# Norm weights applied to rows, operands made in pieces, low-rank products two to a bank

## What is computed

```python
def rms_norm(x, g):
    y = xf * lax.rsqrt(jnp.mean(xf * xf, axis=-1, keepdims=True) + RMS_EPS)
    return (y * g).astype(x.dtype)

p = rms_norm(h, norm_mix_pre) @ w_in                  
r, k, v, wd, ad, gd = split(p_rw + (shift(p_rw) - p_rw) * mu)
w = -softplus(-(w0 + tanh(wd) @ w2)) - 0.5            # low-rank products
a = sigmoid(a0 + ad @ a2);  g = sigmoid(gd) @ g2
# 8 heads, state S[64 x 64]:  S = S*decay + sa (kk*a)^T + v k^T ;  y = S r
y = group_norm_heads(y) * lnx_w + lnx_b               # the recurrent rows
# retention: q, k rotated (rotary), 8 heads, two chunks of 128; group norm per head, silu gate
h = h + rms_norm(merged @ w_out, norm_mix_post)
h = h + rms_norm(conv_ffn(rms_norm(h, norm_ffn_pre)), norm_ffn_post)
# second block: mamba2 mixer, per-layer embedding, shared keys and values
# (kv_norm), window attention (attn_norm), per-layer embedding
```

## Time and profile before

| | |
|---|---|
| median of 3 runs | 992.21 us (991.54 to 994.03) |
| the profiled execution | 992.41 us, span 990.4 us |
| PE busy | 921.5 us (93%), mean granted clock 0.979 |
| DVE busy | 682.0 us (69%) |
| ACT busy | 518.2 us (52%) |
| POOL busy | 62.5 us (6%) |
| PE in the chain that ended last | 63% |
| bytes moved | 135.57 MB, 137 GB/s |

### The profile page before, as it was taken

One profiled execution on the slowest core, in us unless ns is written; L12 is line 12 of the kernel. 1 busy time (PEld: TensorE's weight loads), 2 busy tenths in 40 slices (PEclk: granted clock), 3 DMA queues, 4 the chain that ended last, 5 costly groups with the idle time before them and its releaser, 6 DMA issues.

```text
span 990.4 us, 14250 instructions
## 1 busy us (share of the span) xinstructions
PE 921.5 (93%) x5697; PEld 808.3 (82%) x5697; DVE 682.0 (69%) x936; ACT 518.2 (52%) x745; POOL 62.5 (6%) x65
## 2 busy tenths in 40 slices
PE   4989999999998997999999889989989998999988
PEld 3887898889886876999988689977878786778776
DVE  4569753793488668888873587877556776877654
ACT  4654331232454355666643465865556566467643
POOL 7000420440000000000000000000000000000000
PEclk9899999999999997999999979999999999999999
DMA  9432221222354443656555625543322444542231
GB/s 304 133 128 85 85 87 43 85 86 71 101 187 153 161 156 132 210 179 206 182 201 176 202 91 165 182 130 127 127 75 97 138 159 149 192 137 97 85 101 70
DMA packets 80530, 135.57 MB, mean 137 GB/s; under 512 B 3893, under 2 KB 46225, under 8 KB 80464
## 3 DMA queue, kind: packets, MB, share of 16 engines
q1 hardware_dynamic: 78640, 131.17, 40.2%
q0 software_dynamic: 1824, 3.48, 1.1%
HBM read 133.59 MB, written 1.05 MB: 136 GB/s over the span
## 4 chain that ended last, share of the span: by engine, by line
PE 63%; ACT 6%; DVE 5%; issue 3%; DMA 1%; ACTq 0%; DVEq 0%
PE bank L418 18%; PE bank L420 17%; PE bank L419 17%; PE bank L406 3%; ACT upper L1170 2%; DVE lower L1652 1%; PE bank L833 1%; PE bank L1027 1%; PE bank L842 1%; PE bank L1011 1%; ACT arena L1589 1%; ACT arena L1232 1%; PE bank L643 1%; DVE h L1711 1%; DMA loaded<-in_ffn_w_up 1%
## 5 line engine op out<-in xcount | busy, mean ns | idle before, releaser
L1652 DVE TENSOR_TENSOR lower<-loaded,upper 128x2048 fp32r<-128x2048 f32 (+1 forms) x123 | 279.3, 2276 | 131.5 <-ACT upper L1170 129.5
L1170 ACT ACTIVATE upper<-loaded 128x2048 fp32r<-128x2048 f32 (+1 forms) x123 | 233.7, 1901 | 113.5 <-PE bank L420 94.5
L418 PE MATMUL bank<-xT_upper,upper 128*128 128x256 f32 (+1 forms) x664 | 189.7, 286 | 9.0 <-DVE xT_lower L1693 9.0
L419 PE MATMUL bank<-xT_lower,upper 128*128 128x256 f32 (+1 forms) x664 | 188.1, 283 | 0.0
L420 PE MATMUL bank<-xT_upper,lower 128*128 128x256 f32 (+1 forms) x664 | 187.8, 283 | 0.0
L418 PE MATMUL bank<-upper,xT_upper 128*128 128x512 f32 x352 | 145.9, 414 | 6.2 <-DVE lower L1652 3.5
L420 PE MATMUL bank<-upper,xT_lower 128*128 128x512 f32 x352 | 138.9, 395 | 0.0
L419 PE MATMUL bank<-lower,xT_upper 128*128 128x512 f32 x352 | 138.2, 393 | 0.0
L418 PEld LDWEIGHTS bank<-xT_upper,upper 128*128 128x128 f32 (+1 forms) x664 | 128.7, 194 | 10.9 <-issue 10.8
L418 PE MATMUL bank<-upper,split_arena 128*128 128x512 f32 x296 | 121.2, 410 | 11.6 <-DVE arena L2193 4.7
L419 PEld LDWEIGHTS bank<-xT_lower,upper 128*128 128x128 f32 (+1 forms) x664 | 128.7, 194 | 0.1
(11 more groups left out here) (318 smaller groups left out, 1200.7 us busy)
## 6 DMA issues: line engine op xcount, KB each, us to landing
loaded<-in_w_in SPq DMA_DIRECT2D x27, 1024.0 KB, 5.1
loaded<-in_ffn_w_up SPq DMA_DIRECT2D x22, 1024.0 KB, 5.1
loaded<-in_ssm_in_w SPq DMA_DIRECT2D x20, 1024.0 KB, 5.3
loaded<-in_ffn_w_down SPq DMA_DIRECT2D x11, 1024.0 KB, 4.9
loaded<-in_ssm_out_w SPq DMA_DIRECT2D x8, 1024.0 KB, 4.9
loaded<-in_ple_gate_w SPq DMA_DIRECT2D x8, 1024.0 KB, 5.1
loaded<-in_attn_in_w SPq DMA_DIRECT2D x8, 1024.0 KB, 5.3
loaded<-in_w_branch_ret SPq DMA_DIRECT2D x4, 1024.0 KB, 5.0
```

The source lines that it names most:

```text
L418: mm(out, a[0], b[0], start=start, stop=False)
L419: mm(out, a[0], b[1], start=False, stop=False)
L1170: A(part(upper, PARTS, n), part(loaded, LOADS, n), ACT.Copy).then_inc(uppers, 1)
L1652: TT(part(lower, LOADS, n), part(loaded, LOADS, n), part(upper, PARTS, n).bitcast(F32), sub) \
```

## The change

1. Norms 1 and 2: the weight is broadcast over the partitions by two new transfers (`rowsw`), and applied to the rows, before the transpose (for the first tile by a product of `h` with it beside the sums, for the second within the scaling). `scale` goes; the halves are made straight from PSUM.
2. `pieces` names the banks and the blocks of 128 columns of each transposed tile; rows are scaled in halves, and PE waits for pieces of columns and not for halves of a tile.
3. Norm 0 and the key-value part of norm 4: ACT and DVE make the halves per block, straight from PSUM, with the weight as the column that scales it (`columns_upper`, `columns_lower`). The first unit is loaded and split in two halves, and the first product runs over both column groups half by half (`first_turned`). The square of norm 4 is taken in two halves.
4. The constant table is loaded after four units. The broadcasts of GpSimd's list stand behind its work on the first inverse.
5. Low-rank products of decay and rate: two to a bank, so four banks hold all eight; the gate's four go to four banks; ACT copies the gates before it widens `kroot`. `columns(4)` moves one unit earlier.
6. `L` products between the `m` products; angles in two calls; a rotation in two calls, its sum and weight behind the next level's adds; output copies of `dense` no longer three quarters behind at `L` and at the first scores.
7. The recurrent rows are centred tile by tile, between the right-hand sides and after the first scores; the first output tile's norm moves ahead of `dense("o")`.

The core of the diff:

```diff
+        def pieces(n, i):
+            if n in (3, 5):
+                banks = (2 * i, 2 * i + 1)
+            elif n == 4:
+                banks = (6, 7) if i else (4, 5, 0, 1)
+            elif n == 1:
+                banks = (2, 3, 6, 7) if i else (0, 1)
+            else:
+                banks = (6, 7, 2, 3) if i else (4, 5)
+            m = KT // len(banks)
+            return [(("nT", n, i, p), bank, m * p, m) for p, bank in enumerate(banks)]
...
 PE
+            def first_turned(name, keys):
+                for half in range(2):
+                    pe.wait_ge(lowers, half + 1)
+                    for c in range(2):
+                        for k in range(4 * half, 4 * half + 4):
+                            if c == 0:
+                                xT_ready(0, (5 if k < 4 else 9) + k)
+                            last = mm3(...)
...
+                    for q in range(2):
+                        for name, bank, r, x in (("w", 4, ...), ("a", 6, ...)):
+                            ps = take(pe, (name, q), bank + q)
+                            for e in range(2):
+                                last = mm(ps[:, T * e:T * e + T], ...)
...
-                        lora_product("g", p, 6 + p % 2, lora[:, 1, P * p:P * p + P], lor[:, 1, :])
+                        ps = take(pe, ("g", p), 4 + p)
...
+                    if hd in (3, 5):
+                        o = hd // 5          # the four products of ("L", n, o)
...
-                        if between and half and i == 0:
+                        if between and i and half == 0:
                             between()
...
 SP
-                if n == 2:
+                if n == LOADS:
                     sp.dma_start(consts[:, P:ncols], io["table"][:, P:ncols])
+                if n == 0:
+                    sp.dma_start(dst[:, 0:4, :], src[:, 0:4, :]).then_inc(sem("first_landed"), 16)
+                    sp.wait_ge(sem("x_landed0"), 16)
+                    sp.dma_start(dst[:, 4:8, :], src[:, 4:8, :]).then_inc(unit_landed[0], 16)
...
 GpSimd
             pool.dma_start(h[:, :, :], io["x"]...).then_inc(sem("x_again"), 16)
+            spread_row(rowsw[0], io["norm_ffn_pre"][0], "rowsw_landed0")
             pool.wait_ge(sem("h_ready"), 2)
             spread_row(postw[:, :], io["norm_ffn_post"][0], "postw_landed")
+            spread_row(rowsw[1], io["ssm_norm_w_2"][0], "rowsw_landed1")
...
 ACT
+            def columns_upper(n, x, w, i, first=0, last=4):
+                for key, _, k0, m in pieces(n, i)[first:last]:
+                    ps = full(act, key)
+                    for k in range(m):
+                        A(x[0][:, k0 + k, P * i:P * i + P], ps[:, P * k:P * k + P], ACT.Identity,
+                          scale=pc(w, k0 + k)).then_inc(sem("xT_upper_ready"), 1)
...
                 for i in range(2):
                     post_sums(key, m, i)
+                    if i:
+                        norm_upper(n, xT, (0,))
                     row_sums(n, i)
+                norm_upper(n, xT, (1,))
...
                         elif m == 0 and i == 0:
+                            first_sums(1)
                             root_table()
-                            row_sums(4, 0)
+                            other_sums(0)
+                            split_to("pg01.1", 1)
+                            columns_upper(4, xT2, "kv_norm_w_2", 0)
...
 DVE
             def post_norm(key, m, n, w):
                 post_rows(key, m, 0)
+                ve.wait_ge(sem(f"rowsw_landed{n - 1}"), 16)
+                ve.wait_ge(sem("h_ready"), 2 * n - 1)
+                link(TT(hs[:, 0, :], h[:, 0, :], w, mul))
                 row_scale(n, 0)
                 post_rows(key, m, 1)
-                scale(n, 0, xT, w)
-                row_scale(n, 1)
                 lower_rows(n, 0, xT)
-                scale(n, 1, xT, w)
+                ve.wait_ge(sem("h_ready"), 2 * n)
+                row_scale(n, 1, w)
                 lower_rows(n, 1, xT)
...
+                    if n and 1 < k < 6:
+                        rope_piece(k - 2, True)
                     dense(("t", n, k))
                     if n and k < 5:
-                        rope_piece(k - 1)
+                        rope_piece(k - 1, False)
                     dense(("x", n, k))
                     if n == 0 and k == 1:
                         angles()
+                    if n == 0 and k == 2:
+                        angles_left()
...
                 dense(("rhs", n))
+                if n:
+                    centre_recurrent(0)
...
                 dense(("scores", n))
+                if n == 0:
+                    centre_recurrent(1)
...
+            output_norm(0)
+            dense("o")
             for i in range(2):
                 ps = full(ve, ("yT", i))
```

More of the change, by code:

```diff
@@ L410, in norm_turns @@
                 for i in tiles:
-                    pe.wait_ge(sem("rows_scaled"), 2 * n + i + 1)
-                    for q in range(2):
-                        turns(("nT", n, i, q), (0 if n in (1, 3, 5) else 4) + 2 * i + q, [hs[:, i, P * (4 * q + j):P * (4 * q + j + 1)]
-                                                               for j in range(4)])
+                    for key, bank, k0, m in pieces(n, i):
+                        pe.wait_ge(sem("rows_scaled"), 2 * (2 * n + i) + (2 if k0 + m > 4 else 1))
+                        turns(key, bank, [hs[:, i, P * k:P * k + P] for k in range(k0, k0 + m)])
             def mm3(out, a, b, start, stop):
@@ L454, in turned @@
                     fill(last, keys[c])
+                used(name, key=keys[1])
+            def first_turned(name, keys):
+                ps = [take(pe, keys[c], c) for c in range(2)]
+                n = index[name]
+                w = tiles(part(upper, PARTS, n), n), tiles(part(lower, LOADS, n), n)
+                for half in range(2):
[4 more added lines that the diff above has]
+                                xT_ready(0, (5 if k < 4 else 9) + k)
+                            last = mm3(ps[c][:, 0:T], both(w, every, k, slice(c * P, c * P + P)), both(xT, every, k, every),
+                                       k == 0, k == KT - 1)
+                        if half:
+                            fill(last, keys[c])
                 used(name, key=keys[1])
@@ L1160, in _, with first_upper @@
             A = act.activation
-            split_at = [0]
+            split_at = [1]
+            def first_upper(half):
+                if half == 0:
+                    act.wait_ge(sem("first_landed"), 16)
+                else:
+                    act.wait_ge(unit_landed[0], 16)
+                c = slice(1024 * half, 1024 * half + 1024)
+                A(part(upper, PARTS, 0)[:, c], part(loaded, LOADS, 0)[:, c], ACT.Copy).then_inc(uppers, 1)
             def split_to(name, more=0):
@@ L1277, in _ @@
                 if m == 2:
+                    for q in range(2):
+                        for name, dst in (("w", ld), ("a", av)):
+                            ps = full(act, (name, q))
+                            for e in range(2):
+                                p = 2 * q + e
+                                ins = A(dst[:, p, :], ps[:, T * e:T * e + T], ACT.Sigmoid, bias=pc(f"rw_{name}0", p))
+                            empty(ins, (name, q))
                     for p in range(4):
@@ L1293, in _ @@
                 if m == 4:
+                    for p in range(4):
+                        copy(gT[:, p, :], ("g", p), T)
                     act.wait_ge(sem("knorm_ready"), 1)
@@ L1296, in _ @@
                         .then_inc(sem("knorm_wide"), 1)
-                    for p in range(4):
-                        copy(gT[:, p, :], ("g", p), T)
                 if m == 6:
@@ L1688, in lower_rows @@
+            def scale(n, i, x, w, r0=0):
+                for key, _, k0, m in pieces(n, i):
+                    ps = full(ve, key)
+                    g = cols[:, colat[(w, r0)] + k0:colat[(w, r0)] + k0 + m]
+                    TT(hs[:, i, P * k0:P * (k0 + m)].rearrange("p (a b) -> p a b", a=m),
+                       ps[:, 0:P * m].rearrange("p (a b) -> p a b", a=m), bc(g.unsqueeze(2), P, m, P), mul) \
+                        .then_inc(sem("xT_scaled"), 1)
             def lower_rows(n, i, x):
-                for q in range(2):
-                    xl[0] += 1
+                for key, _, k0, m in pieces(n, i):
+                    xl[0] += m
@@ new lines, in lower_rows, with columns_lower @@
+                    src = full(ve, key)[:, 0:P * m] if n in (1, 2) else hs[:, i, P * k0:P * (k0 + m)]
+                    TT(x[1][c], src.rearrange("p (a b) -> p a b", a=m), x[0][c].bitcast(F32), sub) \
+                        .then_inc(sem("xT_lower_ready"), m)
+                if n in (1, 2):
+                    ve.wait_ge(sem("xT_lower_ready"), 16 * n + 8 * i + 8)
+                for key, _, k0, m in pieces(n, i):
+                    empty(ve.nop(), key)
+            def columns_lower(n, x, w, i, first=0, last=4):
```

(9 more changed lines are left out.)

289 lines of the change are left out of this document (158 added, 131 removed).

## The result

The changed kernel took 965.25 us (median of 5 executions, 962.94 to 973.29), the kernel before 994.03 on the same chip (5, 991.54 to 995.33): a ratio of 0.972, with a 95% interval of 0.969 to 0.975. 960 with a range of 951 to 971 was forecast. The profiled execution is the slowest of the five, 973.29 with a span of 971.4; the others have spans of 961.2 to 963.8.

The account below looks back on a forecast made before the run. TensorE was taken to bound the kernel, busy 921.5 of 990.4 us, so edits pay only where it waits. Ten steps summed to 32.1 us saved from 992.4, giving 960.3 (960 from the median), range 951 to 971.

Parts of the forecast that it names:

- Start: Step 1: first product at 12.8 us instead of 18.76, by splitting half a unit and working in blocks; 6.3 us saved.
- Low-rank: Step 2: eight small products no longer wait for the column copy or for banks to be emptied; 6.0 us saved.
- Gates: Step 3: gate products on four banks instead of two, ending a 2.72 us wait; 3.7 us saved, bounds 1 and 4.
- Masks: Step 4: four-product groups put between the mask products remove waits of 1.00 and 1.38; 0.8 us saved.
- Inverse, scores, end of the recurrent part: Steps 5, 6, 7: waits removed at the inverse, score stage and late weight halves after the recurrent part; 4.0, 1.0, 5.0 us.
- The two norms: Step 8: norms after the feed-forward's input and output; 2.0 us saved twice between second h and first product, 4.0 together.
- Key-value norm: Step 9: blocks replace scaling, upper and lower at the key-value norm, its wait split in three; 1.0 us saved.
- The last: Step 10: row scaling in halves removes the last embedding's 0.36 us wait; 0.3 us saved.
- A: VectorE takes over, blocks and copies ending late in decay, mask and rotation stretches; 8.2 us less, 968; chance 0.20.
- B: TensorE's clock stays at 2.4 GHz at the two norms, where the forecast left it slow; 954 us; chance 0.12.
- C: TensorE's clock falls oftener as one long wait becomes several short ones; 997 us at mean 0.94; chance 0.02.
- D: The blocks do nothing, bank and semaphore order giving the same chains; only steps 2, 3, 8 work; 978 us; chance 0.05.

Follow-up runs that it names:

- after: The profiled execution of the unaltered changed kernel, the slowest of its five: 973.29 us, span 971.4.
- step 2 alone: Kernel before with only low-rank products two to a bank, sigmoids ahead of squares and the fourth column group one projection earlier: 987.88 us, ratio 0.997.
- the repeat: The changed kernel, unaltered, executed and profiled a second time: 963.29 us, ratio 0.972 to the kernel before; profiled span 958.8.
- the undone step: Changed kernel with the four gate products on two banks again: 967.73 us, ratio 0.974 to the kernel before.
- the later table: Changed kernel with the constant table issued after the fifth weight unit instead of after the fourth: 966.39 us, ratio 0.973 to the kernel before.
- the eleven fillers: Changed kernel with 11 identity products filling TensorE's wait at each of norms 1 and 2: 962.60 us, ratio 0.969 to the kernel before.
- the weights on columns: Changed kernel with the weights of norms 1 and 2 on the transposed columns again, in the new pieces: 970.57 us, ratio 0.976 to the kernel before.

## Why the prediction was right, step by step

Steps 1, 5, 6, 9 and 10 have no run of their own: the table places their gains, and their causes are read from the rows. The others were undone or made alone.

**Start (6.3).** Right in size: first product at 11.61 and, in eleven further traces of the changed start, at 11.5 to 13.3 (median of all 12.1), against the 12.8. The gain up to 32.6 is 5.5 to 7.8 in these twelve. How much of it the blocks gave isn't shown: the square of the second x tile also starts sooner, at 5.79 in after against 8.22, but at 6.53 in step 2 alone too, with the old queue.

**Low-rank (6.0, bounds 4 and 6.5).** This is the step that failed in after's trace, and the sum's largest miss in the repeat. The failed terms are the 0.5 of wait (3.01 in after, 1.92 in the repeat, 1.43 alone) and the 8 x 0.14 of the products (2.07 in sixteen passes, 3.92 at the lower clock). That the column copies "move ahead" was read from the code; their cover wasn't costed: they stand behind the fifth unit's split on DVE, that behind the split on ACT, and ACT waits for the unit's transfer (2.73 in after), which the sooner start had pulled up against. PE came 7.3 to 7.8 us sooner, the unit 5.3 to 5.9.

**Gates (3.7).** 2.8, inside 1 to 4, but not for the reason given. The bound by DVE's idle of 3.76 was never reached: the products take 1.54 and not the 0.55 of the sum (eight instructions at 0.216), so PE had 3.0 to win and not 4.0. Of these, 2.04 came from the banks, as the undone step shows, and 0.94 from ACT's order, the wait of 2.72 that is 1.77 there.

**Masks (0.8).** Nothing. I had set PE's 103.00 against DVE's 102.58 and called the 0.4 between them gain; the run shows that it isn't PE's order that sets it.

**Inverse, scores, end of the recurrent part (4.0, 1.0, 5.0).** 4.3, 1.0 and 5.1. Each was read as a row with a wait, its releaser, and the idle time of DVE that could take the moved work; those three held best.

**The two norms (4.0).** Right in sum in six of seven traces (4.1 to 4.9; 6.0 in the repeat), wrong in make-up: 1.57 each by undoing, not 2.0. I let the product start after two transposes, 1.40 behind the first; in PE's order all eight come first, and at the lower clock they take 1.97, so it starts 1.84 behind. What made up for it I had left out: fewer slow matmuls behind the norm. Behind norm 1, 24 matmuls take 3.38 in the repeat and 3.48 in after instead of 4.66, in others 4.0 to 4.5. The shorter slow stretch comes with the second wait's end, as the windows above show; how many matmuls fall into it is scatter, 5 to 16 at norm 1 in the seven traces. The Trainium skill, page "TensorE: Matmul & The Clock Gate", section "What's actually happening" (the prediction names the section behind it), says that the count of slow matmuls varies from run to run, and these traces agree.

**Key-value norm (1.0).** 0.7 and 1.8, with the wait split in five, into 0.61, 0.20, 0.98, 1.26 and 0.87, where three were said. What parts the two traces is the clock around the end of the wait of 1.26: 0.58 from 817 to 821 in after, 1.00 from 807 to 811 in the repeat. The table loads behaved as in the earlier trace rows: in after one takes 1.28 at 811.38, and the next ACT instruction starts at 812.67, 0.01 after it. The Trainium skill, page "ScalarE: Activation LUTs", section "What ACT_TABLE_LOAD costs", would have 2.66 a switch, by which this step was a loss of 1.8; the measurement decides against it here.

**The last (0.3).** 0.0: the wait of 0.36 is gone, the stretch is no shorter.

**Left out of the sum.** The state-space part, put at 0, lost 1.0 to 1.3. In the repeat 0.8 of it stands behind PE's wait of 4.7 there: in the 12 us around the first product behind that wait the mean granted clock is 0.72, against 0.86 in before. Why isn't shown.

**Rivals.** A (968) didn't come, though the median of 965.25 lies nearer to it than to 960: steps 3, 5, 7 and 9 gave 2.8, 4.3, 5.1 and 0.7 to 1.8, where A has 1, 2.5, 3 and -1, and DVE's busy time stayed (682.8 against 682.0). B is true as a mechanism, but needs the wait filled; the change alone does a small part of it. C is refuted, with the mean clock at 0.981 to 0.987 against 0.979. D is refuted by the gains at steps 1 and 5 (7.3 to 7.8 and 4.3). Why after's execution ran 8 to 10 us longer than its fellows is placed by the table (the clock's fall behind a wait of 3.0, the wide spacing, a slow stretch near 920 at a clock of 0.83), but what causes the wide spacing stays open.

## What to carry to other kernels

Read a gain off a wait, its releaser, and the idle time that can take the moved work, and check one more link: what the releaser itself waits for, down to the transfer. An operation order on one engine (all eight transposes first, four banks asked for at once) belongs in the sum as much as durations do. Where PE must wait some 5 us anyway, harmless products that stand ahead of the waiting instruction and end before the wait does are worth the wait's slow aftermath. Where they ended 1.65 late they gave nothing, and behind the wait they cost 2.9 us more than they gave.

## What the runs showed of the hardware

- The same 480 matmuls without a gap took 54.40 or 56.54 us at a granted clock of 1.00. A stretch of 1275 matmuls of the feed-forward (in after from 362.1 to 540.0) took 173.3 us in ten of fourteen traces and 177.9 in four (after, the later table, the eleven fillers, the weights on columns); kernels executed in one group show both.
- Waits of 1.92 (the repeat) and 2.31 (the weights on columns) at 30 to 33 us left the clock at 1.00, one of 3.01 there (after) brought 0.56. Behind a wait of 5.1 eight transposes take 1.97, with the wait filled 1.04.
- Products over 128 rows and 256 fp32 columns are two instructions, which start 0.216 apart at a clock of 1.00 (the gates, the fillers).
- Near 920 us some executions have a stretch at a granted clock of 0.83 (after) that others, with the same code, run at 1.00 (the repeat); it costs 1.6 us.
